# Keys of the first two dilated attention orders copied side by side before the score products

## The reference, cut to what matters

```python
DILATED_PATTERNS = ((128, 1), (512, 4), (2048, 16))
...
    s = jnp.einsum('nrbqhc,nrbkhc->nrbhqk', qs, kb) * ATTN_SCALE
    qi = jnp.arange(band)[:, None]
    kk = jnp.arange(2 * band)[None, :]
    rel = qi + band - kk
    ok = (rel >= 0) & (rel <= band) & ((blk > 0) | (kk >= band))
```

## Time and profile before

| what | value |
|---|---|
| median of 3 runs | 2795.27 us (2792.82 to 2796.08) |
| the profiled execution's own time | 2787.96 us |
| its span, first to last instruction | 2786.0 us |
| mean granted TensorE clock | 0.983 |
| busy share PE, DVE, ACT, POOL | 96%, 75%, 56%, 15% |
| chain that ended last: PE | 77%, of which L2124 (scores) 7% of the span |

### The profile page before, as it was taken

How to read it: one execution, slowest core, us unless ns; L and a number is a source line. 1 busy time by engine, 2 the same in 40 slices (tenths; PEclk the granted TensorE clock), 3 DMA queues, 4 the chain that set the end, 5 groups by cost and what they waited for, 6 DMA issues and landing times.

```text
span 2786.0 us, 44280 instructions
## 1 busy us (share of the span) xinstructions
PE 2677.9 (96%) x15584; PEld 2564.5 (92%) x15584; DVE 2098.0 (75%) x3878; ACT 1554.7 (56%) x3015; POOL 418.3 (15%) x568
## 2 busy tenths in 40 slices
PE   8999999899999999979999899999999999999998
PEld 7899999766788989979999899999999999999998
DVE  7999998688645766789898888888888835365463
ACT  6766776656677754445555555555555534244241
POOL 2344334444201430000000000000000000000000
PEclk9999999899999999989999999999999999999999
DMA  5344444555554448843433234322433275456432
GB/s 180 128 150 168 150 138 142 168 186 194 183 196 147 118 126 309 297 166 126 143 111 110 85 104 151 112 92 98 158 133 102 89 262 191 167 196 228 170 114 95
DMA packets 192439, 430.42 MB, mean 154 GB/s; under 512 B 20980, under 2 KB 117108, under 8 KB 188132
## 3 DMA queue, kind: packets, MB, share of 16 engines
q1 hardware_dynamic: 145312, 367.55, 38.7%
q10 hardware_dynamic: 44676, 51.62, 5.6%
q0 software_dynamic: 2240, 8.52, 0.8%
HBM read 350.47 MB, written 77.17 MB: 153 GB/s over the span
## 4 chain that ended last, share of the span: by engine, by line
PE 77%; DVE 12%; ACT 4%; issue 4%; DMA 3%; SPq 0%; ACTq 0%; POOL 0%; DVEq 0%; POOLq 0%
PE bank L2313 11%; PE bank L2314 10%; PE bank L2315 10%; PE bank L2051 10%; PE bank L2052 10%; PE bank L2053 10%; PE bank L2124 7%; PE bank L2149 2%; PE bank L2136 2%; DVE w_lo L1237 2%; PE bank L2148 1%; DMA stage<-in_w 1%; DVE xT L1245 1%; DVE d L1400 1%; DMA rope<-in_rope 1%
## 5 line engine op out<-in xcount | busy, mean ns | idle before, releaser
L2313 PE MATMUL bank<-b_hi,w_hi 128*128 128x348 f32 x2016 | 654.2, 325 | 32.6 <-ACT u2s L1115 17.6
L2314 PE MATMUL bank<-b_lo,w_hi 128*128 128x348 f32 x2016 | 651.3, 323 | 0.0
L2315 PE MATMUL bank<-b_hi,w_lo 128*128 128x348 f32 x2016 | 651.2, 323 | 0.0
L2313 PEld LDWEIGHTS bank<-b_hi,w_hi 128*128 128x128 f32 x2016 | 382.1, 190 | 35.5 <-issue 31.0
L2314 PEld LDWEIGHTS bank<-b_lo,w_hi 128*128 128x128 f32 x2016 | 381.8, 189 | 0.2 <-issue 0.2
L2315 PEld LDWEIGHTS bank<-b_hi,w_lo 128*128 128x128 f32 x2016 | 381.6, 189 | 0.0
L2051 PE MATMUL bank<-ff_hi,w_hi 128*128 128x416 f32 x960 | 340.4, 355 | 7.2 <-DVE ff_lo L1776 7.2
L2052 PE MATMUL bank<-ff_lo,w_hi 128*128 128x416 f32 x960 | 337.3, 351 | 0.0
L2053 PE MATMUL bank<-ff_hi,w_lo 128*128 128x416 f32 x960 | 335.3, 349 | 0.0
L1146 ACT ACTIVATE w_hi<-stage 128x1024 fp32r<-128x1024 f32 x120 | 126.9, 1058 | 337.9 <-PE bank L2053 307.9
L2051 PE MATMUL bank<-h_hi,w_hi 128*128 128x416 f32 x800 | 286.8, 358 | 19.1 <-DVE h_lo L1250 19.1
(11 more groups left out here) (278 smaller groups left out, 5419.9 us busy)
## 6 DMA issues: line engine op xcount, KB each, us to landing
stage<-in_w SPq DMA_DIRECT2D x404, 512.0 KB, 3.4
past<-in_past SPq DMA_DIRECT2D x32, 1152.0 KB, 6.6
ff_in<-gated_rows SPq DMA_DIRECT2D x15, 1664.0 KB, 10.3
gated_rows<-ucb SPq DMA_DIRECT2D x72, 174.0 KB, 1.9
vb<-out_v SPq DMA_DIRECT2D x48, 256.0 KB, 3.2
attention_rows<-ob SPq DMA_DIRECT2D x32, 264.0 KB, 2.1
oc<-attention_rows SPq DMA_DIRECT2D x16, 528.0 KB, 4.0
hp<-normed_rows SPq DMA_DIRECT2D x3, 2784.0 KB, 11.9
```

Source lines behind the costliest of these rows:

```text
L2313: e.matmul(out, hi, b_hi[j][:, kb], start=begins and kb == 0, stop=False, skip_group_check=True)
L2314: e.matmul(out, hi, b_lo[j][:, kb], start=False, stop=False, skip_group_check=True)
L2315: last = e.matmul(out, lo, b_hi[j][:, kb], start=False, stop=kb == KH - 1, skip_group_check=True)
```

## The change

GpSimd copies each block's 128 keys of all four groups (512 elements on each partition) from `kT` into a quarter of a new buffer `keys_row`, a ring of four blocks in which the slot is n. The scores of orders 0 and 1 take the block's slot, or the slots n - 1 and n, as the moving operand with step 1. Order 2 reads `kT` as before. `keys_row` and `oc` share their place in SBUF, so the first load of `oc` waits until the scores of blocks 0 to 31 are done. The semaphore `qp_zeroed` becomes `keys_copied`: its first two counts are the zeroing of `qp`.

```diff
         qp = [sb(f"qp{i}", [P, JT, 2, P], on=in_p) for i in range(2)]
+        with ExitStack() as in_k:
+            keys_row = sb("keys_row", [P, JT, 4 * P], on=in_k)
+        oc = [sb(f"oc{i}", [P, 2, OS], on=in_p) for i in range(2)]
...
# sync, order 2
                         if y == 0:
+                            e.wait_ge(qk_done, 4 * 32)
                             for s in range(2):
                                 e.wait_ge(os_stored[s], 16 * 16)
...
# gpsimd
+            def copy_keys(b):
+                if b.idx:
+                    e.wait_ge(qk_done, 4 * b.idx - 4)
+                e.tensor_copy(keys_row[:, :, P * b.n:P * b.n + P], kT[:, :, strided(b.first, P, b.dil)]).then_inc(keys_copied, 1)
+
             def body(cur, nxt):
                 y = cur.idx - 32
+                if nxt and nxt.order < 2:
+                    copy_keys(nxt)
                 if cur.order == 0:
...
+            copy_keys(blk(0, 0, 0))
+            e.wait_ge(keys_copied, 3)
             for hd in range(2):
                 rows = slice(HD * hd, HD * hd + HD)
                 ins = e.tensor_copy(smp_q[rows, :, :, hd], qT[rows, :, 0:SMP])
...
# tensor
                 n = 2 * P if b.prev else P
-                keys = strided(b.first - P * b.dil if b.prev else b.first, n, b.dil)
+                if b.order < 2:
+                    if t == 0:
+                        e.wait_ge(keys_copied, 2 + b.idx + 1)
+                    keys = keys_row[:, t, P * (b.n + 1) - n:P * (b.n + 1)]
+                else:
+                    keys = kT[:, t, b.first + P - n:b.first + P]
                 for hd in range(2):
-                    last = e.matmul(bank[t][:, 2 * P * (hd + 1) - n:2 * P * (hd + 1)], qp[b.n % 2][:, t, hd], kT[:, t, keys],
+                    last = e.matmul(bank[t][:, 2 * P * (hd + 1) - n:2 * P * (hd + 1)], qp[b.n % 2][:, t, hd], keys,
                                     start=True, stop=True)
```

More of the change, by code:

```diff
@@ L197, in build @@
         ob = [sb(f"ob{i}", [P, OS], on=in_p) for i in range(2)]
-        oc = [sb(f"oc{i}", [P, 2, OS], on=in_p) for i in range(2)]
         cm = sb("cm", [P, HEADS], on=in_p)
@@ L304, in build @@
         made = sem("made")
-        (a_done, qp_zeroed, q_copied, smp_q_zeroed, qk_done, masked, exp_done, tr_done, pv_done, o_out) = (sem(x) for x in (
-            "a_done", "qp_zeroed", "q_copied", "smp_q_zeroed", "qk_done", "masked", "exp_done", "tr_done", "pv_done", "o_out"))
+        (a_done, keys_copied, q_copied, smp_q_zeroed, qk_done, masked, exp_done, tr_done, pv_done, o_out) = (sem(x) for x in (
+            "a_done", "keys_copied", "q_copied", "smp_q_zeroed", "qk_done", "masked", "exp_done", "tr_done", "pv_done", "o_out"))
         pt_ready = [sem(f"pt_ready{i}") for i in range(2)]
@@ L861, in _ @@
             store_v(JT * CHUNKS - 1, CHUNKS - 1, JT - 1)
-            e.wait_ge(qp_zeroed, 2)
+            e.wait_ge(keys_copied, 2)
             e.wait_ge(roped, 8 * CHUNKS)
@@ L1910, in chunk @@
                         for i in range(2):
-                            e.memset(qp[i][:], 0.0).then_inc(qp_zeroed, 1)
+                            e.memset(qp[i][:], 0.0).then_inc(keys_copied, 1)
                     e.wait_ge(gi_ready, m + 1)
```

## The result

The changed kernel takes 2757.44 us in the median (4 runs, 2756.22 to 2758.97), the kernel before took 2794.05 us in the runs beside it (2791.26 to 2796.08). The ratio is 0.987, with a 95% interval of 0.9853 to 0.9887: 36.6 us less, clear of noise. The forecast was 2757 us.

What follows compares the result with a forecast made beforehand. TensorE was taken to bound orders 0 and 1, with DVE close behind in order 0. Terms -22 (order 0), -21 (order 1), +3 (start) and +2 (clock) sum to -38 us: 2795.3 to 2757 us, range 2744 to 2775.

Steps and rivals of the forecast that it cites:

- The price of a strided tile: TensorE's scores in orders 0 and 1: the strided operand costs 0.92 us with 256 columns, 0.42 us with 128.
- The rival that step 1 out of the new buffer is no faster: Scores gain nothing, only the start's cost remains: 2800 us; chance 0.02 together with a milder form.
- Order 0: -22 us forecast: Bodies 1 to 15: DVE becomes the bound, 154.9 us plus 3.5 idle, so 158.4 instead of 180.4 us.
- the other bound of 30 us: Bodies 2 to 15: without DVE's waits for GpSimd, 133 us instead of 163.0, a gain of 30.
- the load bounds the order: Rival, order 0: `qb` landings grow to 12 us, bodies stay near 12, order 0 gains 5: 2774 us; chance 0.10.
- Order 1: -21 us forecast: Bodies 16 to 31: 25.6 us less strided work, minus 2.9 for ACT waits and 1.7 for body 16.
- The loss to ACT's rows: Order 1, seven bodies: TensorE waits longer at t = 1 for ACT's copy of finished rows, 2.9 us lost.
- 2 us for the clock: TensorE waiting for DVE lets the clock fall more often: 2 us more, between 0 and 8.
- The start: +3 us forecast: First scores wait for GpSimd's first copy, 6.4 us later; body 0's slack takes part: 3 us more.
- The copies: 32 copies on GpSimd at 1.1 us each, ends 0.5 and 3.4, hidden behind its waits: cost zero.
- GpSimd as the bound: Rival, orders 0 and 1: decides from 7.5 us a copy; with 9 us the time is 2842 us; chance 0.03.
- ACT as the bound of order 1: Rival: ACT's busy time plus queue waits end order 1 at 128 us instead of 118: 2767 us; chance 0.12.

Runs made afterwards that it cites:

- the unused copies: Changed kernel with all copies and waits kept, but scores of orders 0 and 1 read `kT` at step 4 and 16 again: 2800.31 us.
- the last version: Changed kernel with block 0 reading `kT`, rows turned at t = 2, and unused products before the softmax waits of bodies 12 and 16: 2737.51 us.
- the later turn: Changed kernel with block 0 reading `kT`, plus TensorE turning finished rows at t = 2 instead of t = 1: 2741.24 us.
- block 0 direct: Changed kernel, but block 0 alone reads its keys from `kT` at step 4, so the first scores wait for no copy: 2751.69 us.
- the filling: Changed kernel with block 0 reading `kT`, plus unused products in TensorE's idle time in order 1: 2745.26 us.
- the doubled copies: Changed kernel, but GpSimd makes every copy twice: 2758.03 us.

## Why the prediction was right

**The price of a strided tile** held: 0.92 us with 256 columns, and the unused copies bring 1.84 back. The rival that step 1 out of the new buffer is no faster fell with it. The sentence of the Trainium skill (SBUF — State Buffer, section Door 1: The DMA port swizzle) that float32 can be strided by 4 for free does not hold for TensorE's moving operand here: order 0, at step 4, gained all it was forecast to gain.

**Order 0: -22 us forecast.** The traces give -23.1 for bodies 2 to 15 and -0.8 for body 1; from the medians it is 16.2 us for order 0 alone plus the start's 5.7, so 22. The step that mattered was to stop at DVE's 154.9 us and not to count the 48 us of PE work. DVE is at 97% after the change, and leaving DVE work out is worth 13.4 us after (11.4 us in bodies 1 to 15) and nothing that can be told before. The meetings of DVE's product with GpSimd's, on which the other bound of 30 us hung, stayed: that product took 1.74 us in the median and 3.24 at most, 1.60 and 3.45 before. That the load bounds the order is shown wrong: without 14 of 16 loads of `qb` it is as long as with them. GpSimd did wait for `qb`, in ten of sixteen bodies, which the text named as a sign against the forecast. It was no such sign: with those loads gone GpSimd waited as long for DVE instead. Another of its signs, a window of order 0 with a clock near 0.5, came too: in body 1, as before the change, and once more:

```profile
680.00:684.00 4.00, 1.97 (x7) 1.73 (x8) 3.00 (x6) 0.99 (x4) 1.25 (x2) 0.50 0.39 140
```

It lies in body 12, with the samples' softmax, in which the kernel before fell to 0.62, and the forecast survived it.

**Order 1: -21 us forecast**, -18.8 by the medians of the kernel that changes order 1 alone, and -14.8 in the profiled pair, where order 1 took 123.9 us and not about 118. The term was a little too large. The price of 25.6 us was right: TensorE's busy time over order 1 is 26.6 us under that of before once the clock stays at 1.00 (the last version). The loss to ACT's rows was counted as 0.42 us in seven bodies; that was right for the wait's growth (0.42 to 0.84), and the later turn confirms the place. What was missing is that this wait and that of body 16 let the clock fall inside order 1. The forecast had 2 us for the clock, between 0 and 8, and looked for it in order 0; with block 0 direct, the filling won 6.4 us back, nearly all in order 1.

**The start: +3 us forecast, 5.7 measured**, near the upper bound of 6.4 (TensorE's wait itself grew by 6.5 us). This step was mis-sized: the middle was taken on the argument that body 0 has slack. It has none behind the first load of the samples: the product that waits for it came 6.5 us later, and body 0 ended 7.5 us later, 1.2 us of either being scatter ahead of the copy.

**The copies** cost 1.08 us each against 1.1 forecast by the row of the same size. The Trainium skill's figure (GPSIMD Engine Reference, section on performance pitfalls) had come to an estimate of 1.2 us; the run shows 1.08. None was waited for but the first. GpSimd as the bound fell with the doubled copies, which leave the total as it was. ACT as the bound of order 1 (128 us) fell too: the later turn brought the same ACT work through in 111.0 us.

So the sum by the medians is -22, -18.8 and +5.7, which is -35.1, and the rest to -36.6 is within what these runs can tell. The forecast's +2 for the clock has no term of its own in it; what the clock cost is inside the others. Forecast was -38 against a median of 2795.3, measured is 2757.4. An order 1 that gained less and a start that cost more, 4.9 us together, stand against those 2 us, a median of before 1.2 us lower, and the rest of 1.5. The hit to half a microsecond is closer than the terms are, and that much of it is luck.

## What to carry to other kernels

Price the operation by its cheap form where the trace already has one (here order 2 had both widths at step 1), then take as the gain only what lies above the next engine's work in the same stretch: 48 us of TensorE's work went, 22 came out. Before a helper engine is put ahead of the first item of a pipeline, see what else that engine must finish first; letting the first item use the slow form won 5.7 us back. When a bound engine begins to wait in short pieces, look at its clock in that stage too, and move a consumer one step later before adding work to fill the gap.

## What the runs showed of the hardware

At the low clock a strided operand costs almost nothing. The first three tiles of block 0 run at a granted clock of 0.50 in both kernels: with step 4 they take 3.07 us, with step 1 2.90 us (above). That is 0.06 us a tile; at the full clock tiles of this width differ by 0.42 us. Put the other way, a strided tile of 128 columns takes 1.07 us at the full clock and a third of 3.07, 1.02 us, at half of it: the clock makes almost no difference to it. What in the chip limits the strided read is not shown.

Copies on GpSimd cost 1.05 to 1.15 us whether they read at step 4 or 16. Of those in the kernel whose copies are unused, one took 2.13 us.

The clock fell in some equal bodies and not in others: in the changed kernel at 800 and at 816 us, and not in the other bodies that turn rows, though each has the same wait of 0.83 to 0.85 us. Which of them it takes differs from kernel to kernel, so a part of the scatter between runs (2756 to 2759 us here, 2788 to 2799 for the kernel before) may come from it; that was not tested.
